# Three-pass projections for cross attention and its memory, and VectorE's small work at other places of the loops over heads

## The reference

```
mem_n = rmsnorm(mem, g_mem)
x = x + mixer(rmsnorm(x, g_mix), ...)                 # gated linear attention + block attention
q = rmsnorm(x, g_cross) @ w_cq                        # 4 heads of 128
k, v = split(mem_n @ w_ckv)                           # memory's keys and values
p = softmax(q k^T / sqrt(128));  x = x + (p v) @ w_co
x = x + hier_moe(rmsnorm(x, g_moe))                   # router, 32 experts of 1024 x 512, 2 per token
x = rmsnorm(x, g_final)
for layer in (0, 1):                                  # second block
    h = rms_norm(x, g_attn)                           # projections dq, dk, dv, sq, sk, sv, gates
    rotate dq, dk; 4 heads of differential attention, each head normed (subln)
    8 heads of stick-breaking attention; merge by sigmoid gates; @ w_out
    x = x + swiglu ffn
return rms_norm(x, norm_final)
```

## Time and profile before

| | us |
|---|---|
| median of 3 runs | 1546.88 (1546.61 to 1547.34) |
| profiled execution, its time | 1545.11 |
| its span, first to last instruction | 1543.3 |
| TensorE busy | 1399.9 |
| VectorE busy | 765.1 |
| ScalarE busy | 588.9 |

### The profile page before, as it was taken

The page is one execution under the profiler, slowest core; times in us unless marked ns, Lnnn a source line. Parts: engine busy times, 40 slices in busy tenths (PEclk is TensorE's granted clock), DMA queues, the critical chain, the costliest instruction groups (busy, mean ns, idle before and its releaser), DMA issues.

```text
span 1543.3 us, 23285 instructions
## 1 busy us (share of the span) xinstructions
PE 1399.9 (91%) x10283; PEld 1155.3 (75%) x10283; DVE 765.1 (50%) x1091; ACT 588.9 (38%) x736; POOL 2.9 (0%) x8
## 2 busy tenths in 40 slices
PE   7999999999777867767899999999999999999998
PEld 5697899754333433433688989999998988999986
DVE  2547664511100100110697678666457767766553
ACT  2454452411100000000445865444343596554343
POOL 0000000000000000000000000000000000000000
PEclk9999999999988988898999999999999999999999
DMA  6653158699999999999834345565534433655640
GB/s 217 224 176 141 55 194 338 241 403 427 427 427 426 426 426 427 427 427 425 299 123 158 125 149 165 182 200 192 205 123 159 169 110 113 206 188 164 218 192 28
DMA packets 116413, 375.03 MB, mean 243 GB/s; under 512 B 7783, under 2 KB 53143, under 8 KB 103767
## 3 DMA queue, kind: packets, MB, share of 16 engines
q1 hardware_dynamic: 112343, 371.23, 62.7%
q0 software_dynamic: 528, 2.04, 0.4%
q10 hardware_dynamic: 3440, 0.25, 0.2%
HBM read 372.44 MB, written 1.06 MB: 242 GB/s over the span
## 4 chain that ended last, share of the span: by engine, by line
PE 66%; DMA 19%; DVE 8%; ACT 4%; issue 1%; ACTq 1%; SPq 0%; DVEq 0%
PE bank L617 29%; DMA ring<-in_w_exp_up 11%; PE bank L859 5%; PE bank L1210 4%; PE bank L661 4%; PE bank L1204 4%; PE bank L633 3%; PE bank L1012 3%; DMA tail_hn<-in_w_exp_up 3%; DMA SZ<-in_w_exp_up 3%; DVE parts L1736 3%; DMA ring<-in_w_in 2%; PE bank L982 2%; PE bank L1039 2%; PE bank L598 2%
## 5 line engine op out<-in xcount | busy, mean ns | idle before, releaser
L617 PE MATMUL bank<-hnr,parts 128*128 128x256 f32 x3888 | 477.8, 284 | 0.2 <-DVE parts L1736 0.2
L617 PEld LDWEIGHTS bank<-hnr,parts 128*128 128x128 f32 x3888 | 470.1, 192 | 4.7 <-issue 4.1
L1736 DVE TENSOR_TENSOR parts<-ring,parts 128x2048 fp32r<-128x2048 f32 x148 | 333.6, 2287 | 106.1 <-ACT parts L1307 105.5
L1307 ACT ACTIVATE parts<-ring 128x2048 fp32r<-128x2048 f32 x146 | 271.5, 1903 | 92.2 <-PE bank L1210 29.2
L1012 PE MATMUL bank<-ring,TMP 128*32 128x512 f32 x608 | 89.7, 743 | 50.1 <-DMA ring<-in_w_exp_up 49.4
L2087 DVE COPY KV<-bank 128x256 f32<-128x256 f32 x16 | 6.8, 424 | 217.6 <-PE bank L999 217.6
L1012 PEld LDWEIGHTS bank<-ring,TMP 128*32 128x32 f32 x608 | 23.3, 132 | 108.7 <-issue 92.7
L617 PE MATMUL bank<-SKr,parts 128*128 128x256 f32 x672 | 81.8, 284 | 0.0
L617 PEld LDWEIGHTS bank<-SKr,parts 128*128 128x128 f32 x672 | 81.1, 192 | 0.1
L859 PE MATMUL bank<-Gr,parts 128*128 128x256 f32 x576 | 72.8, 291 | 4.5 <-DVE Gr L1884 4.5
L859 PEld LDWEIGHTS bank<-Gr,parts 128*128 128x128 f32 x576 | 72.2, 199 | 5.1 <-issue 5.1
(11 more groups left out here) (352 smaller groups left out, 1799.0 us busy)
## 6 DMA issues: line engine op xcount, KB each, us to landing
ring<-in_w_in SPq DMA_DIRECT2D x60, 1024.0 KB, 7.3
ring<-in_w_ffn_in SPq DMA_DIRECT2D x44, 1024.0 KB, 7.4
ring<-in_w_exp_gate SPq DMA_DIRECT2D x19, 2048.0 KB, 38.9
ring<-in_w_exp_up SPq DMA_DIRECT2D x19, 2048.0 KB, 43.4
ring<-in_w_exp_down SPq DMA_DIRECT2D x18, 2048.0 KB, 38.6
ring<-in_w_ffn_out SPq DMA_DIRECT2D x20, 1024.0 KB, 6.0
G<-in_w_exp_gate SPq DMA_DIRECT2D x7, 2048.0 KB, 38.2
tail_hn<-in_w_exp_up SPq DMA_DIRECT2D x7, 2048.0 KB, 42.9
```

Source lines behind the costliest of these rows:

```text
L617: m = mm(b(name)[:, T * half:T * half + T], part(chunk, ws)[:, k, P * mt:P * mt + P], src[xs][:, k, :], start=k == 0 and i == 0, stop=k == ...
L1307: A(parts[:, 2 * (r % 2), 2048 * i:2048 * i + 2048], ring[:, CHUNK[chunk][0], 2048 * i:2048 * i + 2048], ACT.Copy).then_inc(high_made, 1)
L1736: v.tensor_tensor(parts[:, 2 * (r % 2) + 1, at], ring[:, CHUNK[chunk][0], at], parts[:, 2 * (r % 2), at].bitcast(F32), ALU.subtract).then_ ...
```

## The change

All chunks go the split way. Memory's pieces are split before the norm; keys and values are scaled by memory's root when they are read from PSUM, for which the root is turned to tokens (`mr`). The first quarter of the keys' weights is split by VectorE alone. ScalarE's transfers move to SyncE's list. Cross attention's tiles and heads' outputs get high and low parts; `co` begins with three of four heads. The stores are renumbered and filled at other points. In the second block each rotation waits for its own tile; `n_final`'s eight products go in two groups of four behind `diff_logits(2)` and `diff_logits(3)`, and its reciprocal ahead of `diff_norm(1)`; the first of the four head norms moves from head 4 to head 2, and the others one step up. The diff, cut to its core:

```diff
@@ group_plan: order of results in the banks
-    g = ["gains", "mt0", "mt1", "mt2", "mt3", "xt0", "xt1", "xt2", "xt3", "n_mem", "bucket",
-         "kc0", "kc1", "n_mix", "vc0", "vc1", "bj0", "bj1", "bj2", "bj3"]
+    g = ["gains", "mt0", "mt1", "mt2", "mt3", "bucket", "kc0", "kc1", "xt0", "xt1", "xt2", "xt3", "n_mem",
+         "vc0", "n_mix", "mr", "vc1", "bj0", "bj1", "bj2", "bj3"]
...
-SPLIT = [n for n in ALL_CHUNKS if not n.startswith(("ckv", "cq", "co"))]
+SPLIT = list(ALL_CHUNKS)
...
-        stores = ((ring[:, 4], ring[:, 5]), (G[:, 2048:6144], tail_hn[:, :]), (hx[:, :], SZ[:, :]), (ring[:, 0], ring[:, 1]),
+        stores = ((hx[:, :], SZ[:, :]), (G[:, 2048:6144], tail_hn[:, :]), (ring[:, 4], ring[:, 5]), (ring[:, 0], ring[:, 1]),
                   (ring[:, 2], ring[:, 3]))
...
@@ SyncE
-            sp.dma_start(x_tok, ...).then_inc(x_in, 16)        # now ahead of ckv_v
...
                     fetch(slot, wide[slot], cols(w_in, offs[name]), 8)
+                    if name == "qk":     # walr, wau
+                    if name == "vm":     # wr (two), brow (two)
...
-            used(sp, "out0")
+            full(sp, "pb3")
+            fill(0, 1, 1, store_landed[1], slots=(0,))
+            used(sp, "out1")
+            fill(0, 0, 0, store_landed[0], slots=(1,))
+            sp.wait_ge(low_made, 2 * SPLIT.index("cq") + 2)
+            fill(1, 0, 3, store_landed[3], slots=(0,))
+            used(sp, "cq")
+            fill(0, 0, 0, store_landed[0], slots=(0,))
             fill(1, 1, 4, store_landed[4])
-            used(sp, "out1")
-            fill(0, 0, 0, store_landed[0])
-            fill(0, 2, 2, store_landed[2])
-            full(sp, "co3")
-            fill(0, 1, 1, store_landed[1], slots=(0,))
-            used(sp, "cq")
+            sp.wait_ge(low_made, 2 * SPLIT.index("co") + 2)
+            fill(1, 0, 3, store_landed[3], slots=(1,))
             used(sp, "co")
-            fill(1, 0, 3, store_landed[3])
+            fill(0, 2, 2, store_landed[2], slots=(0,))
             full(sp, "ht3")
             fill(0, 1, 1, store_landed[1], slots=(1,))
+            fill(0, 2, 2, store_landed[2], slots=(1,))
...
@@ TensorE
-            linear_f("ckv_k", mem_n, ["kc0", "kc1"], h_at=0)
-            norm_sum("n_mix")
-            linear_t("ckv_v", mem_n, ["vc0", "vc1"])
+            split_by_turns("ckv_k", mem_parts, ["kc0", "kc1"], None)
+            pe.wait_ge(x_in, 16)
+            to_features(x_tok, [f"xt{j}" for j in range(4)])
+            norm_sum("n_mem")
+            split_t("ckv_v", ["vc0", "vc1"], mem_parts, turn_mem_root)   # n_mix and mr between its tiles
...
-            linear_f("cq", hn, ["cq0"], h_at=16)
+            split_by_turns("cq", hn_parts, ["cq0"], (cross_split, 0))
             norm_sum("n_cross")
-            linear_f("cq", hn, ["cq1"], h_at=16, first=1)
+            split_tile("cq", hn_parts, "cq1", 2)
+            split_tile("cq", hn_parts, "cq1", 3)
...
+                for ks in (range(3), (3,)):                # co: heads 0 to 2, then head 3
+                            if j == 0:
+                                emptied(pe, f"co{k}")
+                            for i, (ws, xs) in enumerate(PASSES):
...
-                for name in ("dq0", "dq1", "dk0", "dk1"):
-                    emptied(pe, name + x)
                 for i, (t, name) in enumerate(((dq, "rq"), (dk, "rk"))):
                     for j in range(2):
+                        emptied(pe, f"d{name[1]}{j}{x}")
...
@@ ScalarE
+            emptied(act, "gains")
             act.wait_ge(weight_ready, 1)
             A(both_weight, both_weight, ACT.Sqrt, bias=eps_col).then_inc(weight_root, 1)
+            for j in range(4):
+                full(act, f"mt{j}")
+                for half in range(2):
+                    k = 2 * j + half
+                    A(mem_parts[0][:, k, :], b(f"mt{j}")[:, T * half:T * half + T], ACT.Copy, scale=gain("g_mem", k))
+                A(SQ[:, 512 * j:512 * j + 512], b(f"mt{j}")[:, :], ACT.Square).then_inc(mem_high, 1)
+            A(parts[:, 0, 2048:4096], ring[:, CHUNK["ckv_k"][0], 2048:4096], ACT.Copy).then_inc(high_made, 2)
+            high("ckv_v")
...
+            norm_squares("n_cross", xres, [f"ou{j}" for j in range(4)], cross_beside)   # high copy; high("cq") at j == 1
+            high("co")
             norm_root("n_cross")
...
                 take(f"ct{h}", cprobT[h % 2])
+                if h:
+                    take_oc(h - 1)
+            take_oc(3)
...
@@ VectorE
+            mem_low(0)
+            dve.wait_ge(first_mem_landed, 16)
+            first_weights(0).then_inc(first_quarter, 1)
+            mem_low(1)
+            first_weights(1024).then_inc(low_made, 1)
+            mem_low(2)
+            low("ckv_k", [1])
+            mem_low(3)
...
+            low("ckv_v")
+            for j in range(4):
+                take(f"xt{j}", two(xres, j))
+            v.reciprocal(mem_root, mem_root).then_inc(mem_root_ready, 1)
             for j in range(1, 4):
                 add_squares("n_mix", j)
+            take_scaled("kc0", two(kc, 0), over_tiles(mem_root))
+            take_scaled("kc1", two(kc, 1), over_tiles(mem_root))
+            low("qk", [0])
...
             merge("", 0)                                   # now with cross_low and low("cq") inside
+            cross_low(3)
             add_squares("n_cross", 3)
+            low("co")
...
                 diff_logits(1)
+                if l == 0:
+                    emptied(dve, "n_final")
+                    link(v.reciprocal(final_root, final_root))
                 diff_norm(1)
                 low("sv" + x)
                 take_do(0)
-                if l == 0:
-                    emptied(dve, "n_final")
-                    link(v.reciprocal(final_root, final_root))
-                    for k in range(KT):
-                        v.scalar_tensor_tensor(xres[:, k, :], xres[:, k, :], gain("g_final", k), final_root,
-                                               ALU.mult, ALU.mult).then_inc(h_ready, 1)
                 full(dve, "dt0" + x)
                 diff_logits(2)
+                final_apply(range(4))
                 diff_norm(2)
...
                 diff_logits(3)
+                final_apply(range(4, KT))
                 diff_norm(3)
...
+                    if h == 2:
+                        head_apply(od, ["dn0" + x, "dn1" + x], 0, subs)
...
-                    for i in {4: (0,), 5: (1, 2), 6: (3,)}.get(h, ()):
-                        last = head_apply(od, ["dn0" + x, "dn1" + x], i, subs)
+                    if h in (4, 5, 6):
+                        last = head_apply(od, ["dn0" + x, "dn1" + x], h - 3, subs)
```

More of the change, by code:

```diff
@@ L318, in build @@
         stick = [TMP[:, 384 * i:384 * i + 384] for i in range(4)]
-        qc, oc = view(G, 0, 4, T), view(G, 1024, 4, T)
-        cprob = [view(G, at, TB, T) for at in (2048, 2560, 4096, 4608)]
-        cprobT = [view(G, 3072 + 512 * i, HALF) for i in range(2)]
+        qc = view(G, 0, 4, T)
+        oc_parts = (view(Gr, 1024, 4, T), view(Gr, 0, 4, T))
+        cprob = [view(tail, 512 * i, TB, T) for i in range(4)]
+        cprobT = [view(SQ, 512 * i, HALF) for i in range(2)]
         htok = view(G, 0, TB, D)
@@ L430, in landed @@
             slot, use = CHUNK[name]
-            short = 16 if (slot, use) >= CHUNK["dq.0"] and slot == CHUNK["dq.0"][0] else 0
+            short = sum(16 for n in ("ckv_k", "dq.0") if slot == CHUNK[n][0] and use >= CHUNK[n][1])
             eng.wait_ge(slot_landed[slot], 32 * (use + 1) - short)
@@ L660, in split_t @@
                         for i, (xs, ws) in enumerate(PASSES):
-                            m = mm(b(name)[:, :], hn_parts[xs][:, k, P * tb:P * tb + P], part(chunk, ws)[:, k, :],
+                            m = mm(b(name)[:, :], src[xs][:, k, P * tb:P * tb + P], part(chunk, ws)[:, k, :],
                                    start=k == 0 and i == 0, stop=k == KT - 1 and i == 2)
-                    fin(m, name)
-            def linear_t(chunk, src, names):
-                landed(pe, chunk)
-                w = wide[CHUNK[chunk][0]]
-                for tb, name in enumerate(names):
-                    room(pe, name)
-                    for k in range(8):
-                        m = mm(b(name)[:, :], src[:, k, P * tb:P * tb + P], w[:, k, :], start=k == 0, stop=k == 7)
                     fin(m, name)
@@ L908, in _ @@
             cross_out(3)
-            for h in range(4):
-                emptied(pe, f"co{h}")
-            landed(pe, "co")
-            w = tall[CHUNK["co"][0]]
             def route_logits(ks):
                 for k in ks:
-                    pe.wait_ge(h_ready, 24 + k + 1)
+                    pe.wait_ge(h_ready, 8 * NORMS.index("n_moe") + k + 1)
                     for tb in range(TB):
@@ L1296, in head_roots @@
                             bias=eps_col, scale=1.0 / P), name)
-            for j in range(4):
-                take(f"mt{j}", two(mem_f, j))
             def high(chunk, halves=(0, 1)):
```

(27 more changed lines are left out.)

113 lines of the change are left out of this document (77 added, 36 removed).

## The result

The changed kernel takes 1525.08 us (median of 4 runs, 1524.20 to 1526.06), beside 1547.11 for the kernel before (4 runs, 1546.61 to 1548.95): ratio 0.9858, 95% interval 0.9844 to 0.9872. In the two profiled executions the span falls by 19.6 us, from 1543.3 to 1523.7, against a forecast of 18.9. The 22.0 and the 19.6 differ by single runs: the profiled execution of before took 1545.11 us, 2.0 under the median here, and that of the changed kernel 1525.48, 0.4 above its own.

A forecast was written before the change was run, and what follows sets the result against it. TensorE bounds the kernel except in the experts' stage, paced by DMA of weights. Gains of 7.2 + 5.1 + 3.2 + 3.2 + 0.2 = 18.9 us off 1546.88 give 1528.0 us, range 1521 to 1536.

The forecast's parts named there:

- the rival in which prefetch covers the gap: Experts' stage: it doesn't move with its earlier start; only 6.6 us saved, 1540.3; chance 0.06.
- Part 1: Four projections (`cq`, `co`, memory's keys and values): three passes instead of fp32, 120 ns each, save TensorE 9.8 us.
- the rival of cheaper passes: Four projections: each pass costs less, as the rule of four passes has it; 4.1 us more saved, 1523.9; chance 0.06.
- Part 2: Start of the kernel up to `qk`: `qk` starts 7.2 us earlier than 54.30; bounds 3 to 9.2.
- The ladder: Start: ScalarE's and VectorE's successive steps behind the values' weights landing at 23 us, to `qk`'s second low half at 49.7.
- Part 3: Cross attention to the first expert matmul: 5.1 us gained, 2.3 of it ahead of the scores; bounds 2.5 and 6.5.
- The term of -0.8 for `take_oc`: Cross attention's heads: ScalarE's added copy of each head's output starts the last exponential at 276.2 instead of 275.45 us.
- Parts 4 to 6: Second block: 3.2 us for the final norm's pieces, 3.2 for the first head norm, 0.2 for the rotations.
- part 4: Layer 0, final norm's pieces: moved into VectorE's waits, they remove TensorE's wait for the copy of `sv1`; gain 3.2 us.
- The rival in which the small moves only shift VectorE's lateness: Second block: final norm's pieces and first head norm give nothing; 12.5 us saved, 1534.4; chance 0.12.
- part 5: First head norm, both layers: moving it from head 4 to 2 gains 1.6 us each, 3.2 together; bounds 0 and 4.5.
- The rival of a falling clock: Start: the new 3 us wait lowers TensorE's clock through `qk` and `v`; 1553 at 25 us of low-level work; chance 0.04.

The follow-up runs named there:

- e4: The changed kernel with the first rotations waiting for all four banks of dq and dk again: 1526.11 us.
- e6: The changed kernel with the six small transfers issued by ScalarE ahead of its first computation again, instead of by SyncE: 1527.99 us.
- e5b: The changed kernel with a fourth pass (low part by low part) in memory's keys and values: 1533.60 us.
- e10: The changed kernel with `n_mix` in the queue's free bank, cross heads' outputs copied one head later, and x loaded behind the values' weights: 1524.63 us.
- e5a: The changed kernel with a fourth pass (low part by low part) in `cq` and `co`: 1531.88 us.
- again: The changed kernel run once more, unedited, for its own scatter: 1526.0 us, ratio 0.9873 to the kernel before.
- e9: The changed kernel with x loaded ahead of the keys' weights again: 1526.87 us.
- e8: The changed kernel with `n_mix` in the queue's free bank and each cross head's output copied one head later on ScalarE: 1528.24 us.
- e7: The changed kernel with `co` waiting for all four heads before its first tile: 1527.51 us.
- e3: The changed kernel with the final norm's reciprocal and eight products back behind the low part of sv in layer 0: 1531.75 us.
- e2: The changed kernel with the first head norm back at head 4 (products at heads 4, 5 twice, 6): 1530.69 us.
- e1: The kernel before with only the second block's small moves (first head norm, final norm's reciprocal and pieces, rotations): 1537.48 us.

## Why the prediction was right

**The experts' stage.** An earlier start moved most of it. The stage took 439.96 us before and 440.24 after, with its start 9.5 us earlier in this profile (forecast 12.3), so the rival in which prefetch covers the gap is out. But that profile is a lucky one: in ten of the twelve profiles of the changed kernel and its variants the stage takes 441.1 us or more. In e4, where the start is 12.6 us earlier, as forecast, the stage takes 441.8, and `dq` starts 10.8 earlier. What is lost there is lost on the DMA queue. The windows of 300 to 310 us of before, the changed kernel and e6:

```profile
300.00:310.00 10.00, 9.42 (x58) 8.41 (x56) 7.66 (x41) 5.68 (x8) 1.08 (x2) 0.83 1.00 428
300.00:310.00 10.00, 8.43 (x75) 3.86 (x78) 1.66 (x8) 1.64 (x2) 0.00 (x0) 1.00 0.96 374
300.00:310.00 10.00, 8.59 (x47) 3.82 (x46) 1.10 (x5) 1.61 (x2) 0.00 (x0) 0.63 0.51 206
```

and SyncE's last fill ahead of the experts and the first one behind, in e6:

```profile
291.08 1.03 SPq L500 DMA_DIRECT2D ring<-in_w_exp_down  x1
308.98 0.33 SPq L500 DMA_DIRECT2D hx<-in_w_exp_down  x1
```

Between the two SyncE waits for TensorE to be done with the first store. They are 17.9 us apart in e6, whose experts' stage takes 442.2; 15.0 in e4 (441.8); and 13.0 before and in the first profile (440.0 and 440.2). The granted clock is 0.50 around TensorE's first expert matmul in both e6 and e4, from 300 to 306 us in e6 (it starts at 303.3) and from 300 to 302 in e4 (299.4). The forecast had the queue empty "about when the first expert's stores come free, as now", at a cost of 0, and named a queue that idles longer as a sign of being wrong; the runs show 0.3 to 2.3 us, the 7.6 of e5b aside. How much of that is the clock and how much the new order of the stores was not separated: e10 has a granted clock of 1.00 from 300 to 310 us and still takes 441.1.

**Part 1, the passes.** They take 120 ns each in `cq`, `co` and the keys; a fourth pass costs 0.12 us as well (e5a). The rule of four passes (the Trainium skill, "FP8 and Floating Point Precision", section "TensorE Precision Notes") would put three passes at 0.75 of fp32, as an estimate. Here 5.75 us stand for 6.91, 0.83; the trace does not agree, and the rival of cheaper passes is out.

**Part 2, the start.** 7.52 for 7.2. The ladder was right in its steps: the take of the keys at 34.1 to 36, the second wait, `qk` held by nothing at its start. Two of its reasons were not. The small transfers gave nothing: ScalarE takes up the values' weights at 22.91 us in e6 and at 22.88 without the edit (in "again"). And the move of x, which I had taken as harmless order, is worth 2.1 by the profile (e9; the medians can't tell), since the keys' weights release the first passes. The landing itself came at 21.6 to 22.9, forecast 23, so the sum stood.

**Part 3, cross attention.** 2.3 ahead of the scores, as forecast to 0.1; 2.7 among the heads and `co` (29.31 us before from the scores to the router's last products, 26.63 after), forecast 2.8. The term of -0.8 for `take_oc` is there: the last head's TensorE wait, none before, is 0.65 us. The cure that it suggests is wrong, though: in e8 each copy is one head later, and the same wait is 1.35. Why is open. The 1.6 for `co` with three heads measured 1.3 (e7). What then failed to reach the experts' start is clock: 42.5 us at 0.92 in the changed kernel, 40.5 at 1.00 in e4, for the same instructions.

**Parts 4 to 6.** In layer 0 the pieces, put back one by one, cost 3.43 (e3, forecast 3.2), 1.84 (e2, forecast 1.6) and 0.03 (e4, forecast 0.1): 5.30, of 5.31 measured. That part 4's 3.2 came so near is luck: its wait was priced alone, and what stood against it, 1.3 us of clock lost behind the wait and 1.1 us that the loop over heads asks for again at `ba`, nearly cancels. In layer 1 the head norm is 1.85 and the rotations 0.09; the remaining 0.2 of 2.17 is open. The rival in which the small moves only shift VectorE's lateness is out, though a third of the wait was shifted.

**What was missed.** Above all the merge. I had costed its wait at the wait alone; it also took 1.5 us of clock from the 192 matmuls behind it, in each layer (e1, e2). Of the forecast, the step that is wrong in size is part 5: 3.2 forecast, 6.6 measured. It is hidden in the total since the first block's clock went the other way by about as much (1.2 us up to `out1`, 2.0 behind the scores), in these profiles. The first of the two is not the change: counted from the bias's end, before is at 198.9 and e1, with the same code, at 200.2; the changed kernel is at 200.1, e4 at 198.9. So the total of 19.6 is near 18.9 in part by luck. The rival of a falling clock named this mechanism at the new wait of the start; it did fall there (0.56 from 34.88 to 37.17 us, for 2.29 us of work that took 1.35 in the other profile), but came back ahead of `qk`, and in the other profile, behind a wait of 1.7 us, it did not fall. The Trainium skill, "TensorE: Matmul & The Clock Gate", section "What's actually happening", has the throttled state as the default that activity releases; the falls behind the waits of e2, e3 and e9 agree with it.

**The median.** 22.0 us by the first set of runs, 19.5 by the second (1545.46 to 1526.0). The interval of the second, 17.2 to 22.3 us, holds the profiled 19.6 and the forecast of 18.9; that of the first, 19.8 to 24.1, lies just above both.

## What to carry to other kernels

A wait of TensorE can cost more than its length: here waits of 2.3 us took 1.5 more from the 23 us of dense matmuls behind them, and one of 3.2 took 1.3, while a wait of 2.5 us ahead of `dq` took nothing in most executions and 1.5 in e1. So look at the granted clock behind each wait that an edit removes or adds, and compare busy times of the same matmuls. Put small vector work into the engine's own waits for another engine, not between a result and its reader; the eight products cost 3.4 us at one place and made no wait of TensorE at two others. And when several moves are made at once, put them back one by one, and read each stage: the sum was right here because errors cancelled. If an edit moves the start of a stage that transfers bound, look whether the queue has work up to the first transfer that the stage itself releases.

## What the hardware showed that I had not expected

Two executions of one program differ by 2.6 us of span, and all of it is in the stretch from the scores to `dq`; the granted clock there and up to `out1` is not the same each time. From `qk` to `out1` this stage of the changed kernel took 198.8 to 198.9 us in four of the twelve profiles, at a mean of 0.98, and 200.4 to 200.7 in the others, at 0.97. This is what a study by medians of five cannot see through, and what a window cut at two matmuls can.
